# A hybrid encoder layer step: the front rewritten feature-major, with state space work, attention and norms placed between weight pieces

## The chip, the cores and the metric

The kernel runs on one core of a Trainium2 chip. The metric is the time of one execution on the device in microseconds (us), as the median of several runs. The profile shows one further execution; its times are counted from the start of its span. TensorE is PE in the profile, VectorE is DVE, ScalarE is ACT, GpSimd is POOL and SyncE is SP. SP issues most transfers.

## The reference, cut to what is computed

There are 256 prompt rows and 64 sample rows, 320 in all, of width 2048. Everything is float32.

```python
proj = rms_norm(x, norm1_g) @ w_in                 # 2048 -> 4096: q | k | v | u, 1024 each
q = partial_rope(rms_norm(q, q_norm_g), pos)       # 8 heads, 2 x 64 each; k likewise
p = softmax(q @ k.T / 8, block-causal by chunks of 64)      # twice for each head
o = rms_norm((p[0] - lam * p[1]) @ v, subln_g) * (1 - lam_init)
h = complex diagonal scan over time of (B u)       # 64 groups of 16 channels, 64 states each
y = gelu(Re(C h) + d * u)
s = y * sigmoid(y @ w_glu + b_glu)                 # 1024 -> 1024
x = x + concat(o, s) @ w_out                       # 2048 -> 2048
x = x + peer_ffn(rms_norm(x, norm2_g))             # 8 heads, top 16 of 128 x 128 experts
```

Keys, values and last states are outputs too. The sample rows use 256 cached keys and values and a carried state.

## The kernel before

**Pieces.** All weights stream from memory in blocks of 1 MB (128 partitions x 2048) through `ring`, which has four slots. A block has four pieces of 128 x 512. For each piece ACT rounds the weights to a high part (`high`, L517), a second engine subtracts it from the weights and writes the low part, and PE multiplies with both, since three products of rounded operands (high by high, high by low, low by high) make one of float32 accuracy. `w_parts` holds four pieces, so ACT may be up to four pieces ahead of PE. In the front and in the first section of the experts the low part is made by POOL (`low_parts`, L420); in the later sections by DVE (L771, the line of the helper `tt` through which most DVE operations are recorded).

**Stages of the front, one after the other.** Input product: `x` is loaded by rows (`x_tok`), normalised on ACT and DVE, transposed on PE (L1332) and split into `x_parts`; `dense` (L1363 to L1370) keeps rows of `x_parts` as PE's weights and streams a piece's 512 columns, in 8 matmuls for a piece; 32 blocks. Beside it DVE works out the constants of the state space part (L826 to L925). Attention: heads are transposed (L1320), then 24 units (three row tiles by eight heads) go through scores (L1404 to L1407), mask, maximum and weights on DVE (L771, L996 to L1007), exponentials on ACT (L597), transposed weights (L1421) and values (L1437). In the same stretch PE makes the state space kernels (L1450, L1451) and POOL their output matrices (L440 to L450). State space: `u` comes back from memory by time steps, PE transposes it (L1474), DVE runs the scan, L1508 to L1525 make the outputs, ACT applies gelu and SP turns them by way of memory. GLU and output product: 4 and 16 blocks in `dense`, with transposes ahead of each. Then the second norm by rows (L647 to L651, L785), transposes, and the query product of the expert part (16 blocks, L1548 to L1550, 12 matmuls of 320 columns for a piece).

**Experts.** Three sections, 48, 48 and 32 key rows, each a product with `peer_u`, then with `peer_v` (12 matmuls of 256 columns for a piece). The result is transposed back (L1662), added to the saved residual and stored.

Each engine runs its instructions in the order in which they are written; all waits are on semaphores written out by hand. The turn that sets a piece's speed is this one:

```python
act.activation(w_parts[:, q, 0, :], ring[:, k, 512 * q:512 * (q + 1)], ACT.Copy).then_inc(S["w_hi"], 1)
pool.wait_ge(S["w_hi"], i * (4 * SLOTS) + (4 * k + q + 1))
pool.tensor_tensor(w_parts[:, q, 1, :], ring[:, k, 512 * q:512 * (q + 1)], w_parts[:, q, 0, :].bitcast(F32),
                   ALU.subtract).then_inc(S["w_lo"], 1)
```

Of the kernel before, what the change touches and what calls it, by code (L numbers as in the profile page):

```python
# [55 lines left out]
B_OUT = B_GLU + N_GLU  # L56
B_PQ = B_OUT + N_OUT
# [24 lines left out]
def build(nc, io):  # L82
# [8 lines left out]
    with ctx:  # L91

        ARENA = 43744
# [3 lines left out]

        with ExitStack() as front:
            arena = front.enter_context(nc.sbuf_tensor("arena", [P, ARENA], F32))
            small = front.enter_context(nc.sbuf_tensor("small", [P, 960], F32))  # L100

        with ExitStack() as front:
            xT = front.enter_context(nc.sbuf_tensor("xT", [P, DC, T], F32))[:, :, :]
        with ExitStack() as front:
            front.enter_context(nc.sbuf_tensor("arena_before_xn2T", [P, 12288], F32))
            xn2T = front.enter_context(nc.sbuf_tensor("xn2T", [P, DC, T], F32))[:, :, :]
        experts = sb("experts", [P, 29392])
        x_parts = sb("x_parts", [P, 2, DC, T], F32R)
        w_parts = sb("w_parts", [P, 4, 2, 512], F32R)
        h_parts = sb("h_parts", [P, 2, 2, TP], F32R)  # L110
# [3 lines left out]
        def stat(*dims):  # L114

            n = math.prod(dims)
            used[0] += n
            assert used[0] <= 960, used
            r = small[:, used[0] - n:used[0]]
            return r.rearrange("p (a b) -> p a b", a=dims[0]) if len(dims) == 2 else r  # L120

        def at(word, *dims):

            n = math.prod(dims)
            assert word + n <= ARENA, (word, dims)
            r = arena[:, word:word + n]
# [18 lines left out]
        ssq, var, rstd = stat(NT), stat(NT), stat(NT)  # L145
        nlam = stat(1)
        lam2 = stat(2)
        mx, nb, z, rz = stat(2, 2), stat(2, 2), stat(2, 2), stat(2, 2)
        hs, hv, hr = stat(32), stat(32), stat(32)

        x_tok = at(5120, NT, D)
        proj = at(5120, 4, NT, 1024)
        sq_full = at(17408, D)

        WX = [at(17408, GP, 128), at(21504, GP, 128)]
        tmp_big = at(0, GP, 128)
        bbar = [at(4096, 512), at(4608, 512)]
        PWR, PWI = at(14336, 9, GP), at(14624, 9, GP)
        prm = at(14912, 3, GP)  # L160
        sm_ = [at(15008 + 32 * i, GP) for i in range(11)]
        smi = at(15008 + 32 * 11, GP)
        bcin = at(25600, 4, 512)
        nci = at(27648, 512)
        AJR, AJI = at(28160, 8, GP), at(28416, 8, GP)

        CA = [at(29696, GP, 128), at(25600, GP, 128)]
        tmp_ca = [at(33792, GP, 128), at(37888, GP, 128)]
        k7 = at(42016, 1024)
        Tm = at(33792, STEP, 1024)  # L170
        mask = at(43040, 2, 256)
        dmask = at(43728, 16)

        qkT = at(0, 16, T)
        ckT, cv = at(5120, HEADS, PAST), at(7168, 2, 1024)
        sm = [at(9216, 2, T), at(9856, 2, T), at(28672, 2, T)]
        wT = at(10496, 2, 3, 128)
        o_tok = at(11264, NT, 1024)
        sq_head = at(5120, 2048)
        rt = at(7168, 4, 256)  # L180
        sq_o = at(16384, 1024)

        X = at(0, STEP * 1024)
        dprod = at(6464, GROUPS, SSM_P)
        Xg = at(14336, 2, 1024)
        UG = at(8192, GROUPS, CH)
        FS = at(14336, CH, 2 * GP)
        WTs = at(5440, 2, 512)

        HP = at(0, SEGS * (SEG + 1), 2 * GP).rearrange("p (s c) x -> p s c x", s=SEGS)  # L190
        HCt = at(2880, 2 * GP, CH)
        t1, t2 = at(7488, SEGS, 64), at(7808, SEGS, 64)
        far1, far2 = (at(14336 + 1344 * i, 3 * 7, 64).rearrange("p (s c) x -> p s c x", s=3) for i in range(2))

        pw_r, pw_i, pw_t = at(16384, SEG, GP), at(16640, SEG, GP), at(16896, SEG // 2, GP)
        AR, AN = at(43040, SEG, 2 * GP), at(10752, SEG, 2 * GP)
        Y = at(17408, STEP * 1024)

        y_tok = at(14336, NT, 1024)
        z_tok = at(17408, NT, 1024)  # L200
        bglu = at(20480, 1024)
        x2 = at(0, NT, D)

        xn2 = at(6144, NT, D)
# [34 lines left out]
        x3 = ex(0, 2 * D).rearrange("p (a b) -> p a b", a=2)  # L239
# [8 lines left out]
        xd = x_parts[:, :, :, :].rearrange("p a d t -> p (a d t)").rearrange("p (d c) -> p d c", d=DC)  # L248
        LOW_AT = (384, 512, 320)

        def dense_part(p, j, n):

            t0 = LOW_AT[n] if p else TILES[n][0]
            return xd[:, 4 * j:4 * j + 4, t0:t0 + TILES[n][1]]

        def peer_part(p, j, n):
            t0, r = TILES[n]
            return x_parts[:, p, 4 * j:4 * j + 4, t0:t0 + r]

        fold = at(25600, COLS)  # L260

        def bank(b, n=COLS):
# [3 lines left out]
        names = """consts x0 x1 x2 ssq var std xn tr1 xT x1_hi x1_lo mask ca dk  # L266
            slot0 slot1 slot2 slot3 in_mm in_out in_fold u_saved s5in
# [40 lines left out]
        def _(sp):  # L308
            for n, (t0, r) in enumerate(TILES):
                sp.dma_start(x_tok[0:r, n, :], io["x"][t0:t0 + r, :]).then_inc(S[f"x{n}"], 16)  # L310
# [999 lines left out]
        def _(pe):  # L1310
# [147 lines left out]
            for u in range(units + 1):  # L1458
# [4 lines left out]
                if u:  # L1463
                    values(u - 1)
# [276 lines left out]
```

## Time and profile before

| | us |
|---|---|
| median of 3 runs | 2566.47 (2566.16 to 2568.77) |
| profiled execution, time | 2567.54 |
| profiled execution, span | 2565.7 |
| PE busy / DVE / ACT / POOL | 2341.6 / 1603.1 / 1077.1 / 868.9 |
| first weight piece on PE | at 29.48 |
| input product, end | 316.8 |
| attention, end | 472.9 |
| state space outputs, end | 642.0 |
| GLU and output product, end | 812.7 |
| first matmul of the query product | at 830.55 |
| mean granted TensorE clock | 0.924 |

### The profile page before, as it was taken

The numbers are of one execution on the slowest core, as the hardware profiler recorded it, in microseconds if no ns is written. First come the engines' busy times: TensorE is split into PE (matmuls) and PEld (weight loads), VectorE is DVE, ScalarE is ACT, GpSimd is POOL, SyncE is SP. The second block draws the span as 40 slices with busy tenths as digits, with TensorE's granted clock in tenths as the row PEclk, the third lists the DMA queues.
The fourth block names the chain that finished last, engine by engine and source line by source line (L and its number), as shares of the span: only waits on it lengthen the run. The fifth ranks groups of instructions, "written<-read, shape, count | busy, mean of one in ns | idle before, by whom it ended". The sixth has DMA issues, their size and how long they took to land.

```text
span 2565.7 us, 43286 instructions
## 1 busy us (share of the span) xinstructions
PE 2341.6 (91%) x16878; PEld 2194.2 (86%) x16878; DVE 1603.1 (62%) x2614; ACT 1077.1 (42%) x1994; POOL 868.9 (34%) x621
## 2 busy tenths in 40 slices
PE   5799849759898999898889999999999999999998
PEld 4578647545686999898889999999999999999998
DVE  2921875560212348646757888877767888877866
ACT  3334323211434344454444444444454444444443
POOL 3577750300564568964480111111101111111100
PEclk9899955555898999999999999999999999999999
DMA  4243310200534244456668888888877888888864
GB/s 181 99 151 131 134 58 1 58 2 21 184 132 164 102 145 149 165 181 187 196 219 287 342 327 344 311 313 315 316 283 295 327 344 329 312 312 316 333 207 165
DMA packets 110507, 541.23 MB, mean 211 GB/s; under 512 B 11230, under 2 KB 44430, under 8 KB 48462
## 3 DMA queue, kind: packets, MB, share of 16 engines
q1 hardware_dynamic: 52262, 363.94, 39.6%
q0 software_dynamic: 19632, 137.95, 13.2%
q10 hardware_dynamic: 38496, 37.80, 4.6%
q8 instruction: 71, 1.16, 0.2%
q14 instruction: 46, 0.38, 0.0%
HBM read 508.85 MB, written 27.85 MB: 209 GB/s over the span
## 4 chain that ended last, share of the span: by engine, by line
PE 52%; issue 22%; POOL 20%; DVE 2%; DMA 2%; POOLq 1%; ACT 0%; ACTq 0%; SPq 0%; DVEq 0%
POOL w_parts L420 20%; PE psum L1548 16%; PE psum L1549 16%; PE psum L1550 16%; PE psum L1450 1%; PE psum L1451 1%; PE psum L1437 1%; DVE small L1002 1%; DMA experts<-xs_tmp 1%; PE psum L1404 1%; DVE experts L771 1%; PE psum L1421 0%; DMA arena<-u_tmp 0%; POOLq L419 0%; DMA arena<-in_x 0%
## 5 line engine op out<-in xcount | busy, mean ns | idle before, releaser
L517 ACT ACTIVATE w_parts<-ring 128x512 fp32r<-128x512 f32 x1296 | 817.5, 632 | 1124.0 <-PE psum L1550 846.1
L420 POOL TENSOR_TENSOR w_parts<-ring,w_parts 128x512 fp32r<-128x512 f32 x464 | 654.9, 1421 | 478.4 <-ACT w_parts L517 469.9
L771 DVE TENSOR_TENSOR w_parts<-ring,w_parts 128x512 fp32r<-128x512 f32 x832 | 563.2, 690 | 292.9 <-ACT w_parts L517 292.8
L1548 PE MATMUL psum<-x_parts,w_parts 128*128 128x256 f32 (+1 forms) x2304 | 663.3, 288 | 22.3 <-POOL w_parts L420 14.0
L1549 PE MATMUL psum<-x_parts,w_parts 128*128 128x256 f32 (+1 forms) x2304 | 659.6, 286 | 0.0
L1550 PE MATMUL psum<-x_parts,w_parts 128*128 128x256 f32 (+1 forms) x2304 | 659.6, 286 | 0.0
L1548 PE MATMUL psum<-h_parts,w_parts 128*128 128x256 f32 x2048 | 581.3, 284 | 9.3 <-DVE h_parts L771 9.3
L1549 PE MATMUL psum<-h_parts,w_parts 128*128 128x256 f32 x2048 | 580.9, 284 | 0.0
L1550 PE MATMUL psum<-h_parts,w_parts 128*128 128x256 f32 x2048 | 580.7, 284 | 0.0
L1548 PEld LDWEIGHTS psum<-x_parts,w_parts 128*128 128x128 f32 x2304 | 442.0, 192 | 26.3 <-POOL w_parts L420 16.2
L1549 PEld LDWEIGHTS psum<-x_parts,w_parts 128*128 128x128 f32 x2304 | 442.1, 192 | 0.0
L1550 PEld LDWEIGHTS psum<-x_parts,w_parts 128*128 128x128 f32 x2304 | 441.9, 192 | 0.0
L1548 PEld LDWEIGHTS psum<-h_parts,w_parts 128*128 128x128 f32 x2048 | 394.5, 193 | 9.9 <-issue 6.1
L1549 PEld LDWEIGHTS psum<-h_parts,w_parts 128*128 128x128 f32 x2048 | 394.6, 193 | 0.0
L1550 PEld LDWEIGHTS psum<-h_parts,w_parts 128*128 128x128 f32 x2048 | 394.5, 193 | 0.0
L477 POOL DMA_INDIRECT experts<-in_peer_v,experts x64 | 73.0, 1140 | 481.0 <-DVE experts L1242 394.0
L477 POOL DMA_INDIRECT experts<-in_peer_u_rows,experts x64 | 73.1, 1142 | 451.0 <-DVE experts L1237 430.8
L1363 PE MATMUL psum<-w_parts,x_parts 128*128 128x512 f32 x416 | 169.5, 407 | 25.4 <-POOL w_parts L420 14.2
L771 DVE TENSOR_TENSOR arena<-psum,arena 128x512 f32<-128x512 f32 (+2 forms) x42 | 26.3, 637 | 246.9 <-ACT arena L539 110.8
L1364 PE MATMUL psum<-w_parts,x_parts 128*128 128x512 f32 x416 | 166.8, 401 | 0.0
L1365 PE MATMUL psum<-w_parts,x_parts 128*128 128x512 f32 x416 | 166.4, 400 | 0.0
L1242 DVE SCALAR_TENSOR_TENSOR experts<-experts 128x2048 f32<-128x2048 f32 x63 | 147.8, 2346 | 0.0
(197 smaller groups left out, 2510.1 us busy)
## 6 DMA issues: line engine op xcount, KB each, us to landing
ring<-in_peer_u SPq DMA_DIRECT2D x128, 1024.0 KB, 4.8
ring<-in_peer_v SPq DMA_DIRECT2D x128, 1024.0 KB, 4.9
ring<-in_w_in SPq DMA_DIRECT2D x32, 1024.0 KB, 4.8
ring<-in_w_out SPq DMA_DIRECT2D x16, 1024.0 KB, 4.8
ring<-in_w_pq SPq DMA_DIRECT2D x16, 1024.0 KB, 4.7
g_tmp<-experts ACTq DMA_DIRECT2D x16, 1024.0 KB, 7.4
experts<-g_tmp ACTq DMA_DIRECT2D x16, 1024.0 KB, 7.0
arena<-in_x SPq DMA_DIRECT2D x4, 1024.0 KB, 8.0
```

What stands on the lines that cost most here:

```text
L420: pool.tensor_tensor(w_parts[:, q, 1, :], ring[:, k, 512 * q:512 * (q + 1)], w_parts[:, q, 0, :].bitcast(F32), ALU.subtract).then_inc(S["w ...
L477: pool.indirect_dma_start(rows[b], None, table, bass.IndirectOffsetOnAxis(ap=ids[:, k:k + 1], axis=0)).then_inc(S[f"gr{b}"], 16)
L517: act.activation(w_parts[:, q, 0, :], ring[:, k, 512 * q:512 * (q + 1)], ACT.Copy).then_inc(S["w_hi"], 1)
L771: return dve.tensor_tensor(out, a, b, op)
L1002: dve.tensor_scalar(nb[0:r, b, :], mx[0:r, b, :], -HD ** -0.5, None, ALU.mult).then_inc(S["s_mx"], 1)
L1242: dve.scalar_tensor_tensor(accs, row, coef[:, k:k + 1], accs, ALU.mult, ALU.add).then_inc(S["row_used"], 1)
L1363: pe.matmul(o, xh, w_parts[:, q, 0, :], start=start, stop=False)
L1364: pe.matmul(o, xh, w_parts[:, q, 1, :], start=False, stop=False)
L1365: ins = pe.matmul(o, xl, w_parts[:, q, 0, :], start=False, stop=stop)
L1548: pe.matmul(out, w_parts[:, q, 0, c], moving(0), start=start, stop=False)
L1549: pe.matmul(out, w_parts[:, q, 0, c], moving(1), start=False, stop=False)
L1550: return pe.matmul(out, w_parts[:, q, 1, c], moving(0), start=False, stop=stop)
```

## The change

The front is written anew; the expert part keeps its loops.

- Features lie on partitions. `x` comes in transposed from the host, so that the transposes ahead of products fall away. The first norm's factor is no longer applied to `x`: POOL squares (`sq1`), PE sums over partitions with a matrix of ones (`norm_sums`), and the factor is multiplied in where products leave PSUM (`inputs_out`, `project_out`). The second norm does the same with `norm2_sums`, and scales each feature chunk as the query product's pieces go out.
- The four products (input 128 pieces, GLU 16, output 64) are one run of 208 pieces without a loop. After each piece, each engine does what is written for that piece's number. The low part of all 208 is made by DVE (`front_low`).
- State space work stands behind the query, key and value pieces (numbers 36 to 111), attention behind GLU and output pieces (123 to 163). Of the output product, the half that multiplies the state space result comes first.
- `u` goes to memory and back in runs of 40 numbers (8 loads into `UG`), `y` to memory in runs of 40 (16 stores issued by ACT) and back by POOL.
- Scores are masked by not computing exponentials beyond a chunk: two halves of 64 partitions, four exponentials for a unit of the prompt. They have one pair of banks, so `scores(u)` waits for the exponentials of the unit before.
- The residual is loaded into the expert accumulator `acc` (2 MB, ahead of the two `xs` loads on ACT's queue); `evacuate` adds to it and SP stores it transposed. The 32 transposes and the additions at the end fall away.

```diff
+K7_AT, F_AT, TM_AT, Y_AT, QKT_AT, ATT_AT = 36, 52, 70, 88, 116, 123
+Q_NORM, Y_FILLS, O_NORM, O_TURN = (88, 101), (100, 101, 109, 110, 115, 115), (144, 156, 168), (164, 165, 166, 168, 172, 173)
+        def unit_at(u):
+            return ATT_AT + 3 * u // 2
...
+                if b == 12:
+                    sp.wait_ge(S["u_sv"], 32)
+                    for i in range(STEP):
+                        sp.dma_start(UG[16 * i:16 * i + 16, :, :],
+                                     io["u_tmp"].rearrange("(g n) (i c) -> n i g c", n=SSM_P, c=CH)[:, i]).then_inc(S["ug"], 16)
...
+            act.wait_ge(S["s5in"], 16 * len(S5IN))
+            act.activation(prm[:, 2, :], prm[:, 2, :], ACT.Exp).then_inc(S["s5exp"], 1)
...
+            for p in range(16, 4 * B_PQ + 1):
+                b, q = divmod(p, 4)
+                if p in (139, 147):
+                    k0 = 4 * (p == 147)
+                    for k in range(4):
+                        gate_of_y(k0 + k)
+                        if k:
+                            s_high(k0 + k - 1)
+                    s_high(k0 + 3)
+                high_piece(b, q)
...
+                for u in range(NT * HEADS):
+                    if p == unit_at(u) + 10:
+                        values_out(u)
+                    if p == unit_at(u) + 8:
+                        weights_T_out(u)
+                    if p == unit_at(u) + 4:
+                        exponentials(u)
...
+            def front_low(p):
+                b, q = divmod(p, 4)
+                dve.wait_ge(S["w_hi"], p + 1)
+                tt(w_parts[:, q, 1, :], ring[:, b % SLOTS, 512 * q:512 * (q + 1)], w_parts[:, q, 0, :].bitcast(F32),
+                   ALU.subtract).then_inc(S["f_lo"], 1)
...
+            def weighted_inputs(w):
+                ri, g8 = w // 4, slice(8 * (w % 4), 8 * (w % 4) + 8)
...
+                chain.add(tt(ca_cols(dst), qr, x, ALU.mult))
+                chain(tt(ca_cols(tmp_wx), qi, y, ALU.mult))
+                chain.add(tt(dst, dst, tmp_wx, op))
...
+                if 18 <= p < 34 and p % 2 == 0:
+                    weighted_inputs((p - 18) // 2)
+                if p == 20:
+                    inputs_out(0)
+                if p == 34:
+                    inputs_out(1)
+                if 73 <= p < 73 + SEG:
+                    state_step(p - 73)
+                if p in (82, 83, 84):
+                    carry_inside(p - 81)
+                for x in range(8):
+                    if p == (86 + x if x < 2 else 87 + 3 * x):
+                        output_powers(x)
+                for kind in range(2):
+                    n, late = divmod(p - Q_NORM[kind], 3)
+                    if 0 <= n < NT and late == 0:
+                        head_sums(kind, n)
+                    if 0 <= n < NT and late == 2:
+                        heads_normed(kind, n)
...
+                    if p == unit_at(u) + 6:
+                        head_weights(u)
+                    if p == unit_at(u) + 4:
+                        score_max(u)
+                if p >= 154 and (p - 154) % 8 == 0:
+                    residual((p - 154) // 8)
...
+            def group_outputs(g):
+                pe.matmul(out, Tm[:, g, :], UG[:, g, :], start=True, stop=False)
+                pe.matmul(out, CA[x % 2][0][pr, gp % 4, :], HCt[pr, gp, :], start=False, stop=False)
+                ins = pe.matmul(out, CA[x % 2][1][pr, gp % 4, :], HCt[pr, GP + gp, :], start=False, stop=True)
...
+            for p in range(4 * B_PQ):
+                b, q = divmod(p, 4)
+                pe.wait_ge(S["f_lo"], p + 1)
+                if p < 32:
+                    for k in range(4):
...
+                        ins = input_columns(4 * c + k, dc, q, 128 * k)
...
+                elif b < N_IN:
+                    token_rows((p - 32) // DC, p % DC, q)
+                elif b < B_OS:
+                    gated_columns(c, dc, q)
...
+                if K7_AT <= p < K7_AT + 16:
+                    own_kernels(2 * (p - K7_AT))
+                    own_kernels(2 * (p - K7_AT) + 1)
+                if F_AT + 2 <= p < F_AT + 18:
+                    state_inputs(p - F_AT - 2)
+                if F_AT <= p < F_AT + 16:
+                    state_matrices(p - F_AT)
+                if TM_AT <= p < TM_AT + 14:
+                    kernels_moved(p - TM_AT)
+                if Y_AT <= p < Y_AT + 24:
+                    x, part = divmod(p - Y_AT, 3)
+                    for g in range(3 * part, min(3 * part + 3, 8)):
+                        group_outputs(8 * x + g)
+                for u in range(NT * HEADS):
+                    if p == unit_at(u) + 6:
+                        values(u)
+                    if p == unit_at(u) + 4:
+                        weights_T(u)
+                    if p == unit_at(u):
+                        scores(u)
```

## Rows read from the trace of the kernel before

**Rows 1.** Stretches: length, busy us (instructions) PE, PEld, DVE, ACT, POOL; clock, DMA, GB/s.
```profile
317.00:473.00 156.00, 120.39 (x576) 98.57 (x576) 89.54 (x193) 41.64 (x144) 42.67 (x7) 0.53 0.09 34
473.00:645.00 172.00, 123.52 (x779) 87.87 (x779) 64.24 (x124) 30.08 (x98) 22.70 (x14) 0.53 0.13 31
...
830.50:877.00 46.50, 41.60 (x270) 40.99 (x271) 7.85 (x15) 16.66 (x30) 24.51 (x19) 0.94 0.28 102
```

**Rows 2.** Timeline of PE (start us, us) at full clock: matmuls of 512 and 320 columns.
```profile
71.10 0.40 PE L1364 MATMUL psum<-w_parts,x_parts 128*128 128x512 f32 x1
...
85.84 0.39 PE L1365 MATMUL psum<-w_parts,x_parts 128*128 128x512 f32 x1
...
949.77 0.31 PE L1549 MATMUL psum<-x_parts,w_parts 128*128 128x320 f32 x1
...
955.93 0.31 PE L1549 MATMUL psum<-x_parts,w_parts 128*128 128x320 f32 x1
```

**Rows 3.** Timeline of PE: transposes, float32 matmuls of 128 columns, narrow ones at half clock.
```profile
39.13 1.42 PE L1332 MATMUL psum<-ident,arena 128*128 128x128 f32 x12
...
876.41 2.96 PE L1558 MATMUL psum<-arena 128*128 128x128 f32 x24
...
438.89 0.58 PE L1451 MATMUL psum<-arena 64*128 64x16 f32 x2
439.31 0.58 PE L1450 MATMUL psum<-arena 64*128 64x16 f32 x2
```

**Rows 4.** Stretches, PE alone: length, busy us (instructions), granted clock, DMA, GB/s.
```profile
54.80:58.20 3.40, 3.40 (x10) 0.50 0.54 227
58.20:61.00 2.80, 2.80 (x14) 0.99 0.01 3
...
416.00:448.00 32.00, 32.00 (x153) 0.50 0.00 1
...
1128.00:1280.00 152.00, 129.87 (x1093) 1.00 0.63 188
```

**Rows 5.** Timeline of DVE: low parts, small chained operations, two steps of the scan.
```profile
27.81 1.62 DVE L771 TENSOR_TENSOR x_parts<-xT,x_parts 128x512 fp32r<-128x512 f32 x3
...
66.97 0.65 DVE L839 SCALAR_TENSOR_TENSOR arena<-arena 128x32 f32<-128x32 f32 x3
...
544.67 0.96 DVE L771 TENSOR_TENSOR arena<-arena,small 128x320 f32<-128x320 f32 x3 [0.42 <-DVE arena L771]
...
547.33 0.96 DVE L771 TENSOR_TENSOR arena<-arena,small 128x320 f32<-128x320 f32 x3 [0.42 <-DVE arena L771]
```

**Rows 6.** Groups of DVE instructions: count, busy us, mean ns of one, idle before.
```profile
L771 DVE TENSOR_TENSOR arena<-arena,small 128x1024 f32<-128x1024 f32 x4 | 4.9, 1226 | 0.1
L996 DVE TENSOR_REDUCE small<-arena 128x2 f32<-128x512 f32 x8 | 5.4, 676 | 0.0
```

**Rows 7.** Timeline of POOL and DVE at one moment of the attention.
```profile
342.37 7.53 POOL L444 TENSOR_TENSOR arena<-arena 128x4096 f32<-128x4096 f32 x1
342.41 7.57 DVE L1005 TENSOR_SCALAR arena<-arena,small 128x128 f32<-128x128 f32 x1
```

**Rows 8.** Timeline and groups of ACT: table load, high parts, exponentials.
```profile
10.12 1.28 ACT L488 ACT_TABLE_LOAD   x1 [10.12 <-issue]
...
21.11 2.19 ACT L517 ACTIVATE w_parts<-ring 128x512 fp32r<-128x512 f32 x4 [1.93 <-DMA ring<-in_w_in]
...
L597 ACT ACTIVATE arena<-arena,small 128x256 f32<-128x256 f32 x16 | 8.0, 500 | 11.8 <-DVE small L1002 11.8
```

**Rows 9.** Transfers by line: issuing queue, count, KB each, us from issue to landing.
```profile
g_tmp<-experts ACTq DMA_DIRECT2D x16, 1024.0 KB, 7.4
...
arena<-in_c_im POOLq DMA_DIRECT2D x1, 256.0 KB, 15.8
```

**Rows 10.** Chain that ended last (`xs` load) and timeline of the last stores.
```profile
1345.12 13.64 DMA experts<-xs_tmp
...
2558.79 3.22 SPq L403 DMA_DIRECT2D out_y<-experts  x4
```

More of the change, by code:

```diff
@@ L109, in build @@
         w_parts = sb("w_parts", [P, 4, 2, 512], F32R)
+        with ExitStack() as front:
+            small = front.enter_context(nc.sbuf_tensor("small", [P, 1024], F32))
         h_parts = sb("h_parts", [P, 2, 2, TP], F32R)
@@ new lines, in _, with turn @@
+            load("w_pq", SLOTS, B_PQ + SLOTS)
+            sp.wait_ge(S["xn2"], DC)
+            sp.wait_ge(S["x_sv"], 16)
+            sp.wait_ge(S["x2_rows"], 4)
+            sp.wait_ge(S["s_lo"], 8)
+            sp.dma_start(keys, io["keys"]).then_inc(S["keys"], 16)
+            def turn(source, first, base, i):
+                for s in range(SLOTS):
+                    src = io[source][bass.ds(i * SLOTS + (first + s), 1)].rearrange("o p n -> (o p) n")
+                    name, since = low_of(base + s - SLOTS)
+                    sp.wait_ge(S[name], i * (4 * SLOTS) + 4 * (base + s - SLOTS + 1 - since))
+                    sp.dma_start(ring[:, s, :], src).then_inc(S[f"slot{s}"], 16)
@@ new lines, in norm_sums, with norm_turned @@
+            def norm_sums():
+                pe.wait_ge(S["ones"], 1)
+                pe.wait_ge(S["sq1"], 8)
+                for k in range(8):
+                    ins = pe.matmul(bank(4, T), ones1, sq1[:, 4 * (k // 2) + k % 2, :], start=k == 0, stop=k == 7)
+                ins.then_inc(S["ss1"], 1)
+            def norm_turned():
+                pe.wait_ge(S["consts"], ALL_CONSTS)
+                pe.wait_ge(S["rbt"], 1)
+                for n in range(NT):
+                    ins = pe.transpose(psum[:, 5, 128 * n:128 * n + 128], rb1[:, 128 * n:128 * n + 128], ident[:, :])
+                ins.then_inc(S["rtr"], 1)
@@ new lines, in norm2_sums, with sample_rows @@
+            def norm2_sums(k):
+                if k == 0:
+                    pe.wait_ge(S["ones"], 2)
+                    pe.wait_ge(S["o_lo"], 6)
+                pe.wait_ge(S["sq2"], k + 1)
+                pe.matmul(bank(4, T), ones2, sq2[:, k % 4, :], start=k == 0, stop=k == DC - 1).then_inc(S["ss2"], 1)
+            def sample_rows(c):
+                pe.wait_ge(S["x2_out"], 16 + 4 * c + 4)
+                if c >= 2:
+                    pe.wait_ge(S["x2_rows"], c - 1)
+                for k in range(4):
+                    ins = pe.transpose(psum[0:T_SAMPLE, 5 + c % 2, 128 * k:128 * k + 128], x2T[:, 4 * c + k, T_PROMPT:T], ident[:, :])
+                ins.then_inc(S["x2_tr"], 1)
@@ L1671, in stream @@
     if order is not None:
-        b = b[order]
+        b = np.concatenate([b[c, rows] for c, rows in order])
     return np.ascontiguousarray(b.reshape(-1, P, BLOCK))
@@ L1694 @@
         rope[:r, n, 8:16] = np.sin(ang[t0:t0 + r])
-    mask = np.zeros((P, 2, 256), np.float32)
-    for n in range(2):
-        q_chunk = (np.arange(P) + 128 * n) // 64
-        mask[:, n] = np.where(np.arange(256)[None, :] // 64 <= q_chunk[:, None], 0.0, -1e30)
     dmask = np.zeros((P, SSM_P), np.float32)
```

1817 lines of the change are left out of this document (968 added, 849 removed).

## The prediction

> **What bounds the kernel now.** I read the stretches first, then the chain of waits, then the timelines of single engines. From the query product on, the change leaves the work as it is, so the question is what stands ahead of 830.55 us, the first matmul of the query product. There the stretches show two kinds of stage. In the products (29.5 to 317 and 645 to 813) PE streams at full clock. In attention and state space (317 to 645, 328 us) no weight piece is multiplied at all; the mean granted clock is 0.53, and DVE and ACT are busy for less than 60% [rows 1]. These 328 us are a chain of small steps between engines. The second norm costs 17.8 us ahead of the query product (812.7 to 830.5 in the table), and PE idles on for parts of the 46.5 us after it [rows 1]. The profiled execution took 2567.54 us, 1.1 above the median of 2566.47; I sum against the first and carry the difference over.
>
> **Prices.** A matmul of 512 streamed columns takes (85.84 - 71.10) / 65 = 0.227 us, one of 320 columns (955.93 - 949.77) / 42 = 0.147 [rows 2]. So a query, key or value piece (8 x 512) costs 1.815 us of PE, and any other front piece (12 x 320 in the mean) 1.76. The 208 pieces need 96 x 1.815 + 112 x 1.76 = 371 us. A transpose costs 1.42 / 12 = 0.118, a float32 matmul of 128 streamed columns 2.96 / 12 = 0.247; with 128 columns of weights and few streamed ones it took 0.425 at half clock, so 0.213 at full, since the weights set it [rows 3]. A low part costs DVE 0.54 when the next operation doesn't depend on it, a dependent operation on 32 columns 0.22, a scan step 547.33 - 544.67 = 2.66 [rows 5], an operation on 1024 columns 1.23, a maximum over 512 columns 0.68 [rows 6]. A high part costs ACT 2.19 / 4 = 0.55, an exponential of 256 columns 0.5, a change of table 1.28 [rows 8].
>
> **The front, stretch by stretch.** In each I take the engine with the largest sum, since four buffered pieces even out less than 7 us. With 0.58 for a low part and its wait:
>
> 1. Start: 22 us (29.5 before). ACT now begins with a wait for all seven state space inputs, and every high part is queued behind it. Before, the last of them landed 15.8 us after its issue, beside weights [rows 9]; it now leaves POOL at about 4 us, beside `x` and weights. Then one high and one low part.
> 2. Pieces 0 to 15: DVE. Low parts of `x` and weights 16 x (0.58 + 0.46), some 65 chained small operations at 0.22, six of 512 columns, the norm's factor: 40, and 5 for POOL's squares, behind which DVE has to wait. 45 us; PE needs 32.
> 3. Pieces 16 to 35: DVE. Eight `weighted_inputs` of three operations of 1024 columns = 30, low parts 12, `inputs_out` twice 4.2, the rest 5. 55 us; PE needs 36.
> 4. Pieces 36 to 51: PE. 16 x 1.815 + 64 x 0.213 (`own_kernels`) = 43.
> 5. Pieces 52 to 69: PE. 18 x 1.815 + 64 transposes 7.6 + `state_inputs` about 10 = 50.
> 6. Pieces 70 to 87: DVE. 18 low parts 10, eight scan steps 21, carries 11, the rest 10 = 52, of which it has 2 in hand; PE needs 47. 50 us.
> 7. Pieces 88 to 111: PE 24 x 1.815 + 192 x 0.213 = 84.5. DVE 61 (24 low parts, head norms 34, `output_powers` 12.6). POOL makes the other output matrices, 24 operations of 512 columns, some 31 us. In the trace a DVE operation of 128 columns began as POOL began one of 7.53 us, and took 7.57 [rows 7]: the two take turns. 61 + 31 = 92 is above PE's sum. I take 92.
> 8. Pieces 112 to 122: PE 20 + 48 transposes 6 = 26, and 1 for eight stores by ACT. 27 us.
> 9. Pieces 123 to 163: a chain, not a sum. `scores(u + 1)` waits for the exponentials of unit u. From the end of the piece ahead of `scores(u)`: high part 0.65, low part 0.6, the weights of an earlier unit 0.75 to 0.95, maximum 0.8 to 1.25, exponentials 1.25 to 2.1, handshakes 0.2. That is 4.6 us (first row tile), 5.7 (second), 4.6 (sample), in which PE does one piece and one unit's small matmuls; the second unit of a pair costs about as much and hides two pieces. A pair of units and three pieces take 8.8, 10.8 and 10.3 us, four pairs each: 120. Five more pieces with the last units 10, two sigmoid bursts with their table loads 8, two output norms 9, two residuals 2: 149. The waits of 2 us will cost clock: after such a wait the trace has a stretch at 0.50 though PE was busy throughout it [rows 4]. I add 25. 174 us; PE alone would need 111.
> 10. Pieces 164 to 207: PE. 44 x 1.76 + 11 for transposes and norm sums, a stall of 1 us at each of seven residuals, 3 for the last output norm. 98 us.
>
> Chunk changes with four banks: 5 us. Sum: 22 + 45 + 55 + 43 + 50 + 50 + 92 + 27 + 174 + 98 + 5 = 661. The second norm then takes about 9.5 us (residual 1.5, last square and sums 2, factor with its root 3.5, first chunk out and split 1.5, handshakes 1), so the query product begins at 671 instead of 830.5: **-160**.
>
> **The rest.** The stalls behind the start of the query product (46.5 us for 20 pieces, which need 35 [rows 1]) go, since chunks arrive one by one: -10.5. The `xs` load is on the chain that ended last, 13.6 us [rows 10]; 2 MB instead of 1 now lie ahead of it on its queue, at the price of 1 MB in some 5 us, less the 2 us of scaling that falls away: +3. Sixteen transposes in the first section: +2. At the end 32 transposes and eight additions go; the last store (issued from 2558.79 [rows 10]) leaves about 5 us earlier: -5. Net -160 - 10.5 + 5 - 5 = -170: the execution profiled would take 2397, the median 2396. I say **2396**.
>
> **What SP's queue hides.** Eight loads of 160-byte runs (8192 runs) stand ahead of block 13. Bounded below by nothing (they spread over 16 engines like other transfers), above by the nearest row: 2048 runs of 512 bytes land in 7.4 us [rows 9], so 8192 in 30. Four blocks in the ring cover 16 pieces, 43 us. I take nothing; without the cover it would be up to 30. The stores of `y` are of the same kind, and POOL loads `y` back behind its output matrices; 9 pieces lie between the last store and its use.
>
> **A rule against it.** PE and DVE both work beside POOL in stretch 7. The Trainium skill (SBUF — State Buffer, Who interferes with whom) says that a VectorE instruction with two inputs in SBUF and a GpSimd instruction that reads SBUF exclude each other for the whole instruction. By that rule every low part of stretch 7 can wait for POOL, and 92 stands; without it the stretch would take PE's 84.5. The skill (TensorE: Matmul & The Clock Gate, PE-mode transpose) also says that a transpose does not hold the clock up as a matmul does. By that the second rival below gains.
>
> **The rivals.**
>
> *PE sets the pace throughout.* All float32 work on PE (256 narrow matmuls 54.5, 203 transposes 24, `state_inputs` 10, 14 moves of 512 columns 14, values 12, scores 21.5, norm sums 15) is 151 us; with the pieces 522. From 22 us that ends at 544, with the norm 554, and the time is 2278. For it: DVE's and ACT's sums are near or below PE's from piece 36 on. Against it: DVE's are above up to 35, and one pair of score banks makes a chain. Part of it may come true; I count 2280 to 2345.
>
> *Half clock where PE has little to stream.* Between 416 and 448 us PE was busy for all 32 us, and the clock stayed at 0.50 [rows 4]: narrow float32 work did not raise it. Against it: from 1128 to 1280, where products and float32 matmuls alternate every 6 us, it stayed at 1.00 [rows 4]. If it is at half in stretches 7 and 9, they cost 169 and 223 (PE's 84.5 and 111 doubled, all else hidden) instead of 92 and 174: +126, 2522. I count 2450 to 2550.
>
> *Half clock from piece 36 to 163, once lost: slower than before.* In this stretch weight pieces are 64% of PE's work (230 of 361 us); if that share doesn't bring the clock back, the stretch takes 722 us instead of 436, and the time is 2682. It decides from 170 / 286 = 60% of the stretch at half clock on. Against it: in the attention two pieces in a row at half clock are 7 us of dense streaming, and in the trace the stretch at 0.50 in which PE was busy throughout is followed by one at full clock [rows 4].
>
> *The ring runs dry* behind the short runs: up to +30 and again +20 for `y`: 2396 to 2446.
>
> **How the numbers follow.** My case, 2345 to 2450: 0.52; PE's pace: 0.20; half clock in two stretches: 0.20; the ring, at the upper end: 0.02; half clock throughout: 0.05; no change: 0.01. The range 2300 to 2490 leaves out a third of the second case, a third of the third and the last two, 0.2 in all. A difference of under 0.2% can't be told from none. Faster 0.94, same 0.01, slower 0.05.
>
> **What would show it.** The query product's first matmul at 671 (645 to 725). Stretch by stretch: piece 36 at 122, piece 88 at 265, piece 123 at 385, piece 164 at 560. DVE without idle time in pieces 0 to 35, PE waiting there for DVE's low parts; waits of PE for ACT's exponentials in the attention; a clock above 0.8 over the front. I am wrong if the clock is at 0.5 for most of pieces 88 to 163, if PE waits for `ring`, or if the expert part moves by more than 5 us.

## The result

| us | before | after |
|---|---|---|
| median (runs) | 2566.41 (4) | 2505.78 (4, from 2501.89 to 2515.59) |
| ratio, with its 95% interval | | 0.9768 [0.9738, 0.9798] |
| profiled execution, time and span | 2567.54, 2565.7 | 2503.37, 2501.3 |
| first matmul of the query product | 830.55 | 710.51 |
| query product, its length | 132.3 | 181.6 |
| first section's second product begins | 1348.82 | 1281.39 |
| mean granted TensorE clock | 0.924 | 0.957 |

The change gains 61 us; I had forecast 170 (2396) and a range of 2300 to 2490, which does not hold the time. The front came 120 us earlier instead of 160, the query product, which should have become shorter, became 49 us longer, and the first section lost 14 more. The stretches of the changed kernel, cut at the starts of pieces 0, 36, 88, 112, 123 and 164, then at the query product's first and 21st piece and at the second product of the first section (length, busy us and instructions of PE, PEld, DVE, ACT, POOL; granted clock; DMA share; GB/s):

```profile
25.50:123.20 97.70, 78.88 (x435) 73.23 (x436) 93.08 (x218) 30.58 (x53) 1.33 (x1) 0.93 0.28 95
123.20:275.80 152.60, 145.63 (x894) 109.47 (x892) 87.03 (x161) 55.45 (x92) 18.27 (x10) 0.99 0.42 110
275.80:402.60 126.80, 126.80 (x577) 107.46 (x577) 76.15 (x111) 30.10 (x48) 29.19 (x19) 0.78 0.19 61
402.60:428.40 25.80, 25.71 (x138) 20.93 (x138) 8.80 (x14) 14.92 (x32) 1.85 (x13) 1.00 0.77 225
428.40:601.70 173.30, 133.44 (x746) 112.10 (x744) 97.23 (x223) 97.24 (x288) 0.00 (x0) 0.83 0.27 96
601.70:710.50 108.80, 93.82 (x601) 88.68 (x601) 51.88 (x84) 41.15 (x75) 5.46 (x5) 0.97 0.38 136
710.50:808.50 98.00, 60.26 (x264) 55.00 (x264) 26.85 (x35) 20.49 (x41) 25.36 (x20) 0.68 0.17 65
...
1281.40:1571.40 290.00, 279.41 (x2304) 279.21 (x2304) 224.32 (x348) 135.00 (x238) 35.74 (x31) 0.98 0.82 313
```

Three lines carry the result. The 328 us at clock 0.53 of [rows 1] are gone. But in the third line PE is busy for all of 126.8 us, at a clock of 0.78, where 92 were forecast. And the seventh line, the first 20 pieces of the query product, lasts 98 us, with every engine idle for a third of it or more, where the same 20 pieces took 48.8 before (830.55 to 879.30; the 46.5 of [rows 1] stop ahead of the key scores that stand behind the 20th).

What PE waits for in these two stretches, first 275.8 to 402.6, then 710 to 810 (us in total, times, longest):

```profile
PE psum L1509 <- DVE w_parts L867: 1.2, 1, 1.2
```
```profile
PE psum L1485 <- DVE x_parts L867: 37.7, 15, 2.6
PE psum L1485 <- POOL w_parts L478: 6.4, 1, 6.4
```

In the first PE waits for nothing but 1.2 us ahead of its first piece. In the second it waits for DVE once in each of 15 pieces, and the waits are alike. That is the look of a loop, not of a shortage. The timeline of all engines shows the loop (start us, us; in brackets the idle time before and what ended it):

```profile
713.58 0.47 PE L1487 MATMUL psum<-x_parts,w_parts 128*128 128x320 f32 x1
714.14 0.63 ACT L505 ACTIVATE w_parts<-ring 128x512 fp32r<-128x512 f32 x1 [5.11 <-PE psum L1487]
714.68 0.45 ACT L739 ACTIVATE x_parts<-experts 128x320 fp32r<-128x320 f32 x1
714.85 1.26 POOL L478 TENSOR_TENSOR w_parts<-ring,w_parts 128x512 fp32r<-128x512 f32 x1 [5.19 <-ACT w_parts L505]
715.16 1.29 DVE L867 TENSOR_TENSOR x_parts<-experts,x_parts 128x320 fp32r<-128x320 f32 x1 [4.29 <-ACT x_parts L739]
...
716.61 0.38 PE L1485 MATMUL psum<-x_parts,w_parts 128*128 128x320 f32 x1 [2.56 <-DVE x_parts L867]
...
718.75 0.47 PE L1487 MATMUL psum<-x_parts,w_parts 128*128 128x320 f32 x1
719.26 0.63 ACT L505 ACTIVATE w_parts<-ring 128x512 fp32r<-128x512 f32 x1 [4.13 <-PE psum L1487]
719.80 0.45 ACT L739 ACTIVATE x_parts<-experts 128x320 fp32r<-128x320 f32 x1
```

PE ends a piece (713.58 + 0.47); that frees a place in `w_parts`, so ACT makes the high part of the weight piece four ahead (714.14); only behind that, in ACT's order, stands the high part of the next activation chunk (714.68); DVE makes its low part (715.16); and PE, which had the weights of that piece long ago, begins it (716.61). The next round begins at 719.26: 5.1 us for a piece that PE needs 1.76 for at full clock. From start to start the first 15 pieces take 4.5 to 6.1 us.

### The profile page after: what moved, and what is told of

Its sections match the earlier page's. It is cut to its first block, busy times and chain, and to the rows that moved or that the text cites. A ratio compares the mean times of both kernels' runs of the same rounds, so it can differ in the third digit from the quotient of the medians.

```text
span 2501.3 us, 43312 instructions
## 1 busy us (share of the span) xinstructions
PE 2295.2 (92%) x17069; PEld 2190.8 (88%) x17069; DVE 1681.4 (67%) x2885; ACT 1098.5 (44%) x2058; POOL 575.2 (23%) x447
## 4 chain that ended last, share of the span: by engine, by line
PE 58%; issue 22%; POOL 11%; DVE 5%; DMA 1%; ACTq 1%; POOLq 0%; ACT 0%; DVEq 0%
PE psum L1485 16%; PE psum L1486 16%; PE psum L1487 16%; POOL w_parts L478 11%; DVE experts L867 3%; PE psum L1509 2%; PE psum L1511 1%; PE psum L1510 1%; DVE w_parts L867 1%; PE psum L1593 1%; DMA experts<-xs_tmp 1%; PE psum L1592 1%; ACTq L497 1%; PE psum L1514 1%; PE psum L1515 1%
## 5 line engine op out<-in xcount | busy, mean ns | idle before, releaser
L867 DVE TENSOR_TENSOR w_parts<-ring,w_parts 128x512 fp32r<-128x512 f32 x1040 | 711.2, 695 | 506.7 <-ACT w_parts L505 490.7
L1485 PE MATMUL psum<-x_parts,w_parts 128*128 128x256 f32 (+1 forms) x2624 | 785.6, 299 | 70.8 <-DVE x_parts L867 37.7
L1487 PE MATMUL psum<-x_parts,w_parts 128*128 128x256 f32 (+1 forms) x2624 | 771.9, 294 | 0.0
L1486 PE MATMUL psum<-x_parts,w_parts 128*128 128x256 f32 (+1 forms) x2624 | 771.8, 294 | 0.0
L1485 PEld LDWEIGHTS psum<-x_parts,w_parts 128*128 128x128 f32 x2624 | 513.3, 196 | 90.0 <-POOL w_parts L478 65.4
L1486 PEld LDWEIGHTS psum<-x_parts,w_parts 128*128 128x128 f32 x2624 | 514.6, 196 | 0.7
L1487 PEld LDWEIGHTS psum<-x_parts,w_parts 128*128 128x128 f32 x2624 | 514.1, 196 | 0.0
L478 POOL TENSOR_TENSOR w_parts<-ring,w_parts 128x512 fp32r<-128x512 f32 x256 | 358.4, 1412 | 297.7 <-ACT w_parts L505 289.3
L867 DVE TENSOR_TENSOR experts<-experts 128x256 f32<-128x256 f32 (+9 forms) x329 | 195.6, 605 | 64.2 <-PE psum L1594 31.9
L1423 DVE SCALAR_TENSOR_TENSOR experts<-experts 128x2048 f32<-128x2048 f32 x63 | 147.7, 2345 | 0.0
L1418 DVE SCALAR_TENSOR_TENSOR experts<-experts 128x2048 f32<-128x2048 f32 x64 | 146.3, 2285 | 0.0
L867 DVE TENSOR_TENSOR experts<-psum,experts 128x1024 f32<-128x1024 f32 (+4 forms) x138 | 112.9, 854 | 12.3 <-PE psum L1487 11.9
L1509 PE MATMUL psum<-w_parts,x_parts 128*128 128x512 f32 x192 | 89.9, 468 | 10.0 <-DVE w_parts L867 9.3
```

The costliest lines, as they stand in the source:

```text
L867: return dve.tensor_tensor(out, a, b, op)
L1418: dve.scalar_tensor_tensor(row, row, 1.0, xs, ALU.mult, ALU.mult, accum_out=dots[:, k:k + 1]).then_inc(S["row_used"], 1)
L1423: dve.scalar_tensor_tensor(accs, row, coef[:, k:k + 1], accs, ALU.mult, ALU.add).then_inc(S["row_used"], 1)
L1485: pe.matmul(out, w_parts[:, q, 0, c], moving(0), start=start, stop=False)
L1486: pe.matmul(out, w_parts[:, q, 0, c], moving(1), start=False, stop=False)
L1487: return pe.matmul(out, w_parts[:, q, 1, c], moving(0), start=False, stop=stop)
```

## The experiments

Theories: (A) the start of the query product is that loop on ACT; (B) the sample rows of the experts wait behind the 2 MB of `acc` on their queue; (C) pieces 88 to 111 are long because the clock falls beside narrow float32 matmuls; (D) pieces 16 to 35 are bound by DVE; (E) attention is a chain through one pair of score banks. Each has its rival in the texts below. The first four kernels are single edits of the changed kernel.

**A: splits ahead of the weights.**

```diff
-            for dc in range(DC):
+            def x2_high(dc):
                 act.wait_ge(S["xn2"], dc + 1)
                 act.activation(x_parts[:, 0, dc, :], xn2T[:, dc, :], ACT.Copy).then_inc(S["x2_hi"], 1)
+            for dc in range(4):
+                x2_high(dc)
+            for dc in range(DC):
                 high_piece(*divmod(4 * B_PQ + 4 + dc, 4))
+                if dc + 4 < DC:
+                    x2_high(dc + 4)
```

> Edit: at the start of the query product ACT splits the high parts of the second-normed activations of four row blocks ahead of the weight pieces, instead of one behind each piece; nothing else is changed. Theory (order on ACT): in the changed kernel ACT's high part of activation block dc+1 stands behind its high part of weight piece dc+4, which waits for PE's piece dc, which waits for the split of block dc; so each of the first 16 pieces takes a full round of PE, ACT, DVE, some 5.4 us (98 us for the first 20 pieces). With four splits ahead the pieces run at 1.8 to 1.9 us (DVE 0.54 + 1.29 a piece), 20 pieces in 37 to 45 us: 53 to 61 us less, 2445 to 2453. Rival one (VectorE and GpSimd exclude each other): DVE 1.29 + 0.54 and POOL 1.26 come in turns, 3.1 us a piece: some 37 us less, 2469. Rival two (half clock sets the pace): 3.2 us a piece on PE, 35 us less, 2471. Rival three (the ring: block 5 of the query weights is loaded only when all row blocks are normed): PE waits for ring, gain under 40.

Measured: 2445.18 us, ratio 0.9526 [0.951, 0.9542], 60.6 us below the changed kernel. The first 20 pieces take 39.6 us instead of 98, at a clock of 0.96 instead of 0.68 (the stretch; PE's waits from 715 to 762; then rows of the timelines of POOL and DVE):

```profile
721.80:761.40 39.60, 39.58 (x264) 39.17 (x264) 26.03 (x35) 20.65 (x41) 27.58 (x20) 0.96 0.40 160
```
```profile
PE psum L1491 <- POOL w_parts L478: 6.4, 1, 6.4
```
```profile
736.39 1.57 POOL L478 TENSOR_TENSOR w_parts<-ring,w_parts 128x512 fp32r<-128x512 f32 x1 [0.39 <-ACT w_parts L505]
736.73 1.58 DVE L873 TENSOR_TENSOR x_parts<-experts,x_parts 128x320 fp32r<-128x320 f32 x1
738.15 1.32 POOL L478 TENSOR_TENSOR w_parts<-ring,w_parts 128x512 fp32r<-128x512 f32 x1 [0.19 <-ACT w_parts L505]
738.24 1.58 DVE L1302 SCALAR_TENSOR_TENSOR experts<-experts,small 128x320 f32<-128x320 f32 x1
739.75 0.48 DVE L873 TENSOR_TENSOR x_parts<-experts,x_parts 128x320 fp32r<-128x320 f32 x1
```

So A holds, and the other three rivals fall. Half clock was an effect of the loop: it went with it. DVE and POOL do get in each other's way (a low part of 320 columns takes 1.58 when it begins inside one of POOL's, at 736.73, and 0.48 when none is running, at 739.75), but with four splits in hand PE no longer sees it. And PE waited only once, 6.4 us ahead of the first piece, not for `ring`.

**B: sample rows ahead of `acc`.**

```diff
-                            act.dma_start(acc, io["x_tmp"][:, :, 0:TP]).then_inc(S["acc_in"], 16)
                             for half in range(2):
                                 act.dma_start(xs[64 * half:64 * half + 64, :], io["xs_tmp"]).then_inc(S["xs_in"], 16)
+                            act.dma_start(acc, io["x_tmp"][:, :, 0:TP]).then_inc(S["acc_in"], 16)
```

> Edit: ACT issues the two loads of the sample rows (xs, 2 x 512 KB) ahead of the load of acc (2 MB) instead of behind it. Theory (queue order): the sample rows landed 24 us after their issue since 2 MB lie ahead of them on the same queue; PE waited for hidden low parts twice, 8.4 and 10.6 us, because DVE's wait for the rows stands ahead of the low parts. In front they land in about 11 us, as before the change: the second wait goes, 11 to 13 us less, 2493 to 2495. Rival (the loads are slow because of the gathers and weight blocks that share the DMA engines): the rows still take over 20 us, gain under 3. acc is first read at the next section, so its own delay costs nothing by either.

Measured: 2495.73 us, ratio 0.9738 [0.9689, 0.9787]. That is 10 us below the changed kernel, but its interval overlaps that one's, so the whole time does not decide. The stretch does: from the end of the first section's first product to the end of its second it took 298.7 us in the changed kernel (1272.67 to 1571.34, starts of the last matmuls), 284.4 here (1272.67 to 1557.07) and 285.5 before (1342.57 to 1628.07). Transfers (KB each, median us from issue to landing), and PE's waits from 1270 to that end, first of the changed kernel, then of this one:

```profile
experts<-x_tmp ACTq DMA_DIRECT2D x1, 2048.0 KB, 22.1
...
experts<-xs_tmp ACTq DMA_DIRECT2D x2, 512.0 KB, 24.3
```
```profile
PE psum L1485 <- DVE h_parts L867: 19.0, 2, 10.6
```
```profile
experts<-x_tmp ACTq DMA_DIRECT2D x1, 2048.0 KB, 30.0
...
experts<-xs_tmp ACTq DMA_DIRECT2D x2, 512.0 KB, 7.6
```
```profile
PE psum L1485 <- DVE h_parts L867: 6.3, 1, 6.3
```

The rows land in 7.6 us instead of 24.3, though the same gathers and weight blocks are loaded at that time, and of PE's two waits (19.0 us) one of 6.3 is left. B holds, the rival falls.

**C: wider matmuls in the group outputs.** PE is given more to do; the columns that are too many fall on places that the next group overwrites.

```diff
-                out = psum[:, 4 + fill % 4, CH * (gp % 12):CH * (gp % 12) + CH]
-                pe.matmul(out, Tm[:, g, :], UG[:, g, :], start=True, stop=False)
...
+                n = min(3, 12 - gp % 12, GP - gp, GROUPS - g)
+                out = psum[:, 4 + fill % 4, CH * (gp % 12):CH * (gp % 12 + n)]
+                flat = lambda ap: ap.rearrange("p a b -> p (a b)")
+                pe.matmul(out, Tm[:, g, :], flat(UG[:, g:g + n, :]), start=True, stop=False)
...
```

> Edit: each of the 192 narrow float32 matmuls of the group outputs streams up to 120 columns instead of 40; the 80 further columns fall on places of the same bank that the next groups overwrite, so the result is the same. Theory (clock): pieces 88 to 111 took 126.8 us with PE busy throughout and a granted clock of 0.6 to 0.8 because PE streams so little in them; with wide matmuls the clock stays near 1.00 and the stretch takes 24 x 1.815 + 192 x 0.22 to 0.247 = 86 to 91 us: 36 to 41 us less, 2465 to 2470, although PE is given more to do. Rival one (the clock falls because of what lies ahead, or because of float32 as such): clock unchanged, 192 matmuls a little longer: 4 to 10 us more, 2510 to 2516. Rival two (the step in my prediction, DVE and POOL in turns set the stretch): no change within 4 us.

Measured: 2491.05 us, ratio 0.9699 [0.9683, 0.9715]: 14.7 us below the changed kernel, less than half of what I expected, and both rivals are out by sign or size. The stretch of pieces 88 to 111:

```profile
278.20:389.50 111.30, 111.30 (x577) 89.34 (x577) 76.07 (x111) 30.20 (x48) 29.19 (x19) 0.98 0.22 69
```

The clock is 0.98 instead of 0.78, as the theory has it; the size was wrong because the price was. The other traces agree: with 40 columns (A, B, D and the first try of E) the stretch took 122.2 to 135.8 us at 0.72 to 0.82, with up to 120 (the three later kernels that have this edit) 111.1 to 114.3 at 0.96 to 0.99. In the changed kernel's timeline of PE, nine narrow matmuls ahead of a piece at full clock, and six at half:

```profile
328.32 0.31 PE L1592 MATMUL psum<-experts 128*128 128x40 f32 x2
328.56 0.41 PE L1593 MATMUL psum<-experts 64*128 64x40 f32 x2
...
330.95 0.50 PE L1509 MATMUL psum<-w_parts,x_parts 128*128 128x512 f32 x1
...
335.07 0.65 PE L1592 MATMUL psum<-experts 128*128 128x40 f32 x2
...
338.23 0.79 PE L1509 MATMUL psum<-w_parts,x_parts 128*128 128x512 f32 x1
```

From 328.32 to 330.95 are 0.29 us for each of nine, from 335.07 to 338.23 are 0.53 for each of six. With up to 120 columns nine take 3.03 us at full clock, 0.336 each. A weight piece between narrow matmuls takes 1.95 us there (310.47 to 312.42) instead of 1.815. So at full clock the changed kernel's stretch would have cost 24 x 1.95 + 192 x 0.29 = 102.5 us: of its 126.8, some 24 are the clock's. The wide matmuls give back those 24 and take 192 x 0.046 = 9, which comes to the 111.3 measured. That the width of these matmuls makes the difference is shown for this stretch; what in it the clock goes by, these runs do not tell.

**D: low parts of pieces 16 to 35 by POOL.** In each of the three places that name the order of low parts (POOL, PE's wait, SP's wait for a free slot) the pieces 16 to 35 get a semaphore of their own:

```diff
+            for p in range(16, 36):
+                b, q = divmod(p, 4)
+                pool.wait_ge(S["w_hi"], p + 1)
+                pool.tensor_tensor(w_parts[:, q, 1, :], ring[:, b % SLOTS, 512 * q:512 * (q + 1)], w_parts[:, q, 0, :].bitcast(F32),
+                                   ALU.subtract).then_inc(S["p_lo"], 1)
...
-                front_low(p)
+                if not 16 <= p < 36:
+                    front_low(p)
```

> Edit: the low parts of pieces 16 to 35 are made by POOL, which is idle there, instead of DVE. Theory (my step for pieces 16 to 35: DVE is the bound): DVE's 55 us lose 20 x 0.58 = 11.6, and nothing else is late: 8 to 11 us less, 2495 to 2498. Rival (the Trainium skill, SBUF - State Buffer, Who interferes with whom: a VectorE instruction with two SBUF inputs and a GpSimd one that reads SBUF exclude each other): DVE's remaining 43 and POOL's 20 x 1.26 = 25 come in turns, 68 us instead of 55: about 10 to 13 us more, 2516 to 2519.

Measured: 2510.84 us, ratio 0.9796 [0.9761, 0.9832], not to be told from the changed kernel. Pieces 16 to 35 took 56.5 us against 55.2. Both expectations fail, and the rows show why they cancel: the stretch in the changed kernel and here, the changed kernel's DVE, then this one's DVE (timeline, and groups from 68 to 98) and POOL:

```profile
68.00:123.20 55.20, 40.89 (x226) 37.44 (x225) 52.81 (x89) 12.56 (x20) 0.00 (x0) 0.91 0.28 94
```
```profile
67.60:124.10 56.50, 35.86 (x227) 34.15 (x225) 54.64 (x65) 12.66 (x21) 33.27 (x18) 0.85 0.31 114
```
```profile
68.93 3.61 DVE L867 TENSOR_TENSOR experts<-experts 128x1024 f32<-128x1024 f32 x3
```
```profile
69.39 11.25 DVE L872 TENSOR_TENSOR experts<-experts 128x1024 f32<-128x1024 f32 x5
```
```profile
L872 DVE TENSOR_TENSOR experts<-psum,experts 128x256 f32<-128x256 f32 x4 | 2.6, 658 | 0.0
L872 DVE TENSOR_TENSOR experts<-experts 128x64 f32<-128x64 f32 x4 | 1.4, 362 | 0.1
```
```profile
68.34 28.06 POOL L440 TENSOR_TENSOR w_parts<-ring,w_parts 128x512 fp32r<-128x512 f32 x15
```

An operation of 1024 columns took 2.25 us beside POOL instead of 1.20, and a low part on POOL 1.87 instead of 1.26. DVE's operations with an input in PSUM (256 columns, 0.66) kept their time, and those of 64 columns in SBUF took 0.36 instead of 0.28. The turns cost DVE 13 us (56.5 against 55.2 - 11.6) and not POOL's whole 25, as the rival had it: POOL's 20 low parts grew by some 12 (20 x 0.61) meanwhile. DVE is the bound there all the same: it was busy for 54.6 of 56.5 us without its low parts.

**E: the attention's chain, shorter and longer.** The first try was on the changed kernel itself:

```diff
-                    chain.add(dve.tensor_reduce(mx[of, u % 3, :], score_banks(u)[of, :, 0:kk], AX.X, ALU.max))
+                    chain.add(dve.tensor_reduce(mx[of, u % 3, :], score_banks(u)[of, :, 0:16], AX.X, ALU.max))
```

> Edit: in the attention the maximum that DVE takes of each unit's scores runs over the first 16 columns alone, not over all 64 to 320; left out is the rest of the maximum, which only shifts the exponent of a quotient. Nothing else is changed. Theory (my step for pieces 123 to 163: the one pair of score banks makes a chain of matmul, maximum, exponentials, so PE waits 33 us for ACT's exponentials): each of 24 units' chain loses 0.6 to 0.9 us: 14 to 20 us less, a few more if the clock rises, 2484 to 2492. Rival (the stretch is set by the sums of ACT and DVE behind weight pieces, or by PE at its lowered clock): under 5 us less, 2501 to 2506.

Measured: 2499.44 us (2485.32 to 2514.20), ratio 0.9756 [0.9715, 0.9798]: undecided. In its profiled execution the stretch took 160.2 us instead of 173.3, but the runs spread over 29 us. Therefore the base was made quieter first.

**A, B and C together.**

> Edit: the kernel after the change with three edits together: four splits ahead at the start of the query product, sample rows ahead of acc on ACT's queue, and group outputs that stream up to 120 columns. They lie in different stretches, so their gains should add: 60.6 + 10.1 + 14.8 = 85 us less than the changed kernel's 2505.8: 2420, 5.7% below the kernel before. If two of them share a cause (a clock that comes up anyway once PE no longer waits), 2430 to 2440.

Measured: 2420.15 us (2416.48 to 2421.64), ratio 0.9424 [0.9409, 0.944]. The gains add (60.6 + 10.1 + 14.7 = 85.4; measured 85.6), and this version beats both kernels: 146 us below the one before, 86 below the changed one.

**C with 80 columns** (`min(2, ...)` in place of `min(3, ...)`, on this base).

> Edit: as the kernel with three edits, but the group outputs stream up to 80 columns instead of 120. Theory (price and clock apart): a narrow matmul took 0.29 us at full clock with 40 columns, 0.51 at half, and 0.336 with 120 at full; with 80 columns at full clock it should take about 0.30, so if the clock stays at 1.00 pieces 88 to 111 take 24 x 1.815 + 192 x 0.30 = 101 us instead of 111, 7 to 9 us less than with 120: 2411 to 2413. Rival: at 80 columns the clock falls in parts of the stretch, as it did with 40: equal or up to 15 us more than with 120 columns.

Measured: 2424.47 us (2419.16 to 2428.04), ratio 0.945 [0.9434, 0.9466]. Not better: the stretch took 114.0 us at a clock of 0.93, against 111.3 at 0.98 with 120 columns. The clock did not stay at 1.00, and the theory's 101 us were not reached. But another trace with 120 columns has 114.3 at 0.96, and the intervals overlap: whether 80 columns are worse than 120 stays open.

**E again, on the base with three edits**, in both directions. In the second kernel each maximum is followed by the same one once more, into a place that is overwritten later:

> Edit: the kernel with three edits, and in the attention the maximum over the first 16 columns alone (left out: the rest of the maximum). The kernel with the short maximum alone ran in too wide a spread to tell; on this base the spread is some 5 us. Theory (a chain through the one pair of score banks sets pieces 123 to 163): what the maximum loses, 8 x 0.35 + 8 x 0.9 + 8 x 0.45 = 13.6 us, comes off the time in full: 2404 to 2409. Rival (sums of ACT or DVE, or PE at its granted clock, set the stretch): under 5 us less, 2415 to 2420.

> Edit: the kernel with three edits, and in the attention every maximum is taken twice, the second one ahead of the same wait. Theory (chain): each unit's chain grows by its maximum, 8 x 0.74 + 8 x 1.28 + 8 x 0.72 = 22 us more: 2438 to 2446. Rival (DVE is busy for only 97 of 174 us in the stretch, so more work on it is hidden): under 5 us more, 2420 to 2425.

Measured: 2407.21 us, ratio 0.9377 [0.9364, 0.939], and 2436.66 us, ratio 0.9482 [0.9466, 0.9499], against 2420.15: 12.9 less and 16.5 more. The stretch of pieces 123 to 163 with three edits, with the short maximum and with two maxima, each in a trace of its own:

```profile
417.40:589.00 171.60, 129.88 (x745) 109.82 (x743) 97.21 (x223) 97.49 (x288) 0.00 (x0) 0.86 0.27 97
```
```profile
412.80:574.10 161.30, 127.98 (x746) 108.10 (x744) 82.55 (x223) 97.56 (x288) 0.00 (x0) 0.86 0.29 103
```
```profile
420.10:609.40 189.30, 136.12 (x746) 114.65 (x744) 115.95 (x263) 97.65 (x288) 0.00 (x0) 0.81 0.25 88
```

DVE is busy for little more than half of the stretch, yet 14.7 us less on it shorten the stretch by 10.3, and 18.7 more lengthen it by 17.7 (at a clock of 0.81 instead of 0.86, which is part of it). An engine that is idle for almost half the time and passes on 70% and 95% of what is done to it stands in a chain: E holds, with the first time inside what I expected of a chain and the second 1 us under it. Doing without the wait itself (scores of two units in the two banks at once) was not tried: PE would write a bank that ACT is reading.

## Why the prediction was wrong, step by step

| step (us) | forecast | measured |
|---|---|---|
| 1, start: piece 0 at | 22 | 25.5 |
| 2 and 3, pieces 0 to 35 | 100 | 97.7 |
| 4, 5, 6, pieces 36 to 87 | 143 | 152.6 |
| 7, pieces 88 to 111 | 92 | 126.8 |
| 8, pieces 112 to 122 | 27 | 25.8 |
| 9, pieces 123 to 163 | 174 | 173.3 |
| 10, pieces 164 to 207 | 98 | 97.7 |
| chunk changes, in the stretches | 5 | |
| second norm | 9.5 | 11.1 |
| query product, against before | -10.5 | +49.3 |
| `xs` load | +3 | +13.2 |
| 16 transposes | +2 | +0.9 |
| end | -5 | -6.3 |

**The query product: the step that failed.** "The stalls behind the start of the query product (...) go, since chunks arrive one by one: -10.5." I counted what the loop over chunks takes away and did not follow ACT's order inside it. There stood the clue: `high_piece(4 * B_PQ + 4 + dc)` is behind `x2_hi(dc)` on ACT, it waits for PE's piece `dc`, and `x2_hi(dc + 1)` is behind it. It is the kind of wait that I had asked for everywhere else: what is queued behind the waiting instruction. The size of the step without the loop was right: in the kernel with splits ahead the query product takes 123.1 us, where I had 121.8 (132.3 - 10.5). This step makes 60 of the 106 us by which the profiled execution missed its 2397, and none of my rivals named it.

**Step 7: mechanism and price both wrong.** I took 92 because DVE's 61 and POOL's 31 would come in turns. PE waited for nothing but 1.2 us ahead of the stretch's first piece: its own sum was above theirs. That sum I had at 84.5, from 0.213 us for a narrow matmul, half of a value at half clock [rows 3]. At full clock the group outputs, one with 128 rows of weights and two with 64 in turn, cost 0.29, and the pieces between them 1.95, so 102.5; the own kernels of step 4, with 128 rows only, cost 0.20 (130.52 to 131.33 for four). The other 24 us are the clock. That was my rival of half clock, with the price of 169 for the stretch too high: the clock moved between its levels, 0.78 in the mean, and it came in stretch 7 but not beyond what I had added in stretch 9. The measured time lies in the 2450 to 2550 that I had counted for this rival; that is chance, since the larger part of the miss is the query product's. Transposes did not take the clock down: pieces 52 to 69, with 64 of them between weight pieces, ran at 1.00.

**Steps 4 to 6: sizes.** 9.6 us more. A weight piece that stands between other kinds of matmul takes 1.91 us in pieces 38 to 52 and 2.01 to 2.04 in most of pieces 54 to 77 (173.86 to 175.89 in one) instead of 1.815, which no row of mine held; and PE waits for DVE ahead of pieces 37 and 87, 2.6 us each, and 1.2 ahead of 88.

**The `xs` load: mis-sized.** I gave 2 MB ahead of it in its queue 5 us, by the price of a 1 MB block. `acc` takes 256 of every 320 columns of `x_tmp`, runs of 1 KB, and took 22.1 us. I had priced short runs for `UG` and `y` and not here, where they were on the chain. But the runs are only one part of it. The DMA queues of ACT, of the gathers and of SP from its issue to its landing (1274.3 to 1296.4; packets, MB, share of the 16 engines' time):

```profile
q10 hardware_dynamic: 2174, 2.88, 47.7%
q0 software_dynamic: 432, 3.15, 34.8%
q1 hardware_dynamic: 158, 1.16, 13.7%
```

A MB cost ACT's queue 40 to 50% more of that time than it cost the others (47.7 / 2.88 against 34.8 / 3.15 and 13.7 / 1.16), but as much of the time went to the other two, which my price of a single block left out. No run parts the two causes.

**Right, with the reason shown:** pieces 0 to 35 (DVE busy for 93.1 of 97.7 us, PE waiting for its low parts) and attention (E: the chain). That the chain makes 149 us of the attention and the clock (granted 0.83) my added 25 is not shown; only the sum is, and that it came out so close may be luck. The output product and the end came out in size, without an experiment of their own; the smaller misses at the start and in the second norm were not followed up. The ring did not run dry: no engine is shown waiting for it from piece 0 to 710.5, and the eight loads of `UG` landed in 7.6 us (median). Of the signs that I had named, the clock over the front held (0.90 in the mean up to 710.5), and so did the query product's first matmul (710.5, in 645 to 725); pieces 123 and 164 began 43 and 42 us later than I had said; and one spoke against me: the expert part behind the query product, without its end, moved by 12.6 us, not by less than 5.

**The rule against it.** The Trainium skill (SBUF — State Buffer, Who interferes with whom) says that a VectorE instruction with two SBUF inputs contends with a GpSimd one that reads SBUF, and that the port pair they share is an exclusive lock. The traces agree: POOL's low part of 714.85 ends at 716.11, and DVE's, begun at 715.16, ends at 716.45 after 1.29 us, where it takes 0.48 alone (in A). But I used it as a sum of two engines, and the sum counts only where one of them is the bound. In stretch 7 neither was; in D the rule held and cost what the relief gave.

## What to carry to other kernels

Where one engine refills a ring of buffers and also prepares the other operand, write down its order and ask of each wait what stands behind it: an operand that is prepared behind a refill which waits for its own consumer makes a loop. Here a lead of four steps, as many as the ring has places, opened it; a shorter one was not tried. A stretch in which all engines idle alike and one wait recurs with the same length can be such a loop. Price a transfer by its runs and by what is loaded beside it, and a small matmul from a row of the same shape at the same clock.

## What the hardware showed that I had not expected

- More work on PE took less time: 192 matmuls of up to 120 columns instead of 40 shortened their stretch from 126.8 to 111.3 us, at a clock of 0.98 instead of 0.78, although PE was busy without a gap in both.
- A float32 matmul of 40 columns costs 0.29 us at full clock where weights of 128 and of 64 rows take turns, 0.20 with 128 rows only (32 columns); tripling the columns adds 0.046.
- A DVE operation of 1024 columns with its inputs in SBUF took 2.25 us beside a busy POOL instead of 1.20, while POOL's took 1.87 instead of 1.26.
